# The sliding-window keys, values and first queries as a fifth pair of the last FoX period

## What is computed

```python
h = rmsnorm(x); z = h @ w_in          # FoX q, k, v, f | SWA q, k, v | gates g_fox, g_swa
# branch A (FoX): 8 heads of 64, causal, logits + sum of log forget gates
o_A = softmax(q @ k.T * SCALE + cum_q - cum_k) @ v
# branch B (SWA): 8 query heads, 2 key/value heads, a band of 3 chunks of 64, sinks, relative bias
o_B = sink_softmax(q @ k.T * SCALE + bias) @ v
merged = sigmoid(g_fox) * (o_A @ w_proj_fox) + sigmoid(g_swa) * (o_B @ w_proj_swa)
x = x + rmsnorm(merged @ w_o)         # then a ConvFFN over 2816 features
```

## Time and profile before

| | |
|---|---|
| median of 3 runs | 1749.28 us (1748.65 to 1751.57) |
| the profiled execution | 1747.95 us |
| its span | 1746.0 us, mean granted clock 0.967 |
| PE busy | 1616.0 us (93%) |
| DVE / ACT / POOL busy | 982.8 / 434.3 / 577.6 us |
| DMA | 122.88 MB, mean 70 GB/s |

### The profile page before, as it was taken

The page is one execution under the profiler, slowest core; times in us unless marked ns, Lnnn a source line. Parts: engine busy times, 40 slices in busy tenths (PEclk is TensorE's granted clock), DMA queues, the critical chain, the costliest instruction groups (busy, mean ns, idle before and its releaser), DMA issues.

```text
span 1746.0 us, 24406 instructions
## 1 busy us (share of the span) xinstructions
PE 1616.0 (93%) x9375; PEld 1504.1 (86%) x9375; DVE 982.8 (56%) x1846; ACT 434.3 (25%) x914; POOL 577.6 (33%) x312
## 2 busy tenths in 40 slices
PE   5979999988889798967899999999999999999996
PEld 5879999988679798857787998998989989989895
DVE  6756757677432474758645465545445455454556
ACT  4133434345211153532223210100101101001013
POOL 6322213121113313116232333432543444324443
PEclk9989999999989999888999999999999999999998
DMA  5422212221334211124533111111211111112115
GB/s 183 83 78 62 74 49 76 61 66 34 109 100 164 67 46 53 42 78 145 186 109 99 28 49 34 51 48 36 60 36 48 48 36 49 47 36 60 48 37 101
DMA packets 129614, 122.88 MB, mean 70 GB/s; under 512 B 7453, under 2 KB 116377, under 8 KB 129537
## 3 DMA queue, kind: packets, MB, share of 16 engines
q1 hardware_dynamic: 93513, 66.38, 13.1%
q10 hardware_dynamic: 34824, 51.13, 9.4%
q0 software_dynamic: 1200, 4.33, 1.4%
HBM read 94.00 MB, written 27.92 MB: 70 GB/s over the span
## 4 chain that ended last, share of the span: by engine, by line
PE 82%; DVE 12%; DMA 2%; issue 1%; ACT 1%; POOL 0%; SPq 0%; ACTq 0%; DVEq 0%; POOLq 0%
PE bank L682 17%; PE bank L683 17%; PE bank L684 17%; PE bank L688 6%; PE bank L690 6%; PE bank L689 6%; PE bank L714 4%; PE bank L835 2%; DVE m L1972 1%; DVE ssb L1727 1%; DVE ssb L1711 1%; PE bank L806 1%; PE bank L805 1%; DVE m_l L1956 1%; DMA gm<-d_mfox 1%
## 5 line engine op out<-in xcount | busy, mean ns | idle before, releaser
L575 POOL TENSOR_TENSOR ring_h<-raw,att 128x1024 fp32r<-128x1024 f32 x108 | 207.7, 1924 | 1011.8 <-PE bank L684 833.6
L682 PE MATMUL bank<-m_h,ring_h 128*128 128x352 f32 x1056 | 340.7, 323 | 0.7 <-DVE m_l L1524 0.7
L683 PE MATMUL bank<-m_l,ring_h 128*128 128x352 f32 x1056 | 338.6, 321 | 0.0
L684 PE MATMUL bank<-m_h,ring_l 128*128 128x352 f32 x1056 | 338.4, 320 | 0.0
L576 POOL TENSOR_TENSOR ring_l<-raw,ring_h 128x1024 fp32r<-128x1024 f32 x108 | 290.0, 2686 | 8.5
L682 PE MATMUL bank<-ht_h,ring_h 128*128 128x352 f32 x840 | 280.4, 334 | 0.2 <-DVE vqn L1535 0.2
L684 PE MATMUL bank<-ht_h,ring_l 128*128 128x352 f32 x840 | 274.4, 327 | 0.0
L683 PE MATMUL bank<-ht_l,ring_h 128*128 128x352 f32 x840 | 274.0, 326 | 0.0
L682 PEld LDWEIGHTS bank<-m_h,ring_h 128*128 128x128 f32 x1056 | 198.1, 188 | 1.2 <-DVE m_l L1524 0.8
L683 PEld LDWEIGHTS bank<-m_l,ring_h 128*128 128x128 f32 x1056 | 198.4, 188 | 0.3
L684 PEld LDWEIGHTS bank<-m_h,ring_l 128*128 128x128 f32 x1056 | 198.0, 188 | 0.0
(11 more groups left out here) (280 smaller groups left out, 2670.7 us busy)
## 6 DMA issues: line engine op xcount, KB each, us to landing
raw<-in_w_up SPq DMA_DIRECT2D x44, 512.0 KB, 3.9
raw<-in_w_in SPq DMA_DIRECT2D x35, 512.0 KB, 4.0
raw<-in_w_down SPq DMA_DIRECT2D x22, 512.0 KB, 3.6
d_gate<-gst ACTq DMA_DIRECT2D x48, 176.0 KB, 1.9
gm<-d_gate ACTq DMA_DIRECT2D x8, 528.0 KB, 4.2
d_mfox<-mst ACTq DMA_DIRECT2D x8, 528.0 KB, 2.9
gm<-d_gate ACTq DMA_DIRECT2D x24, 176.0 KB, 2.5
gm<-d_mfox ACTq DMA_DIRECT2D x24, 176.0 KB, 2.9
```

The lines of the kernel that those rows point to most:

```text
L575: order.link(nc.gpsimd.tensor_tensor(high, src, zero.to_broadcast(list(src.shape)), ALU.add))
L682: nc.tensor.matmul(out, wh, xh, start=start, stop=False)
L683: nc.tensor.matmul(out, wh, xl, start=False, stop=False)
L684: return nc.tensor.matmul(out, wl, xh, start=False, stop=stop)
```

## The change

The SWA keys, values and queries 0 take the place of a fifth pair: `KEYS`, `VALUES` and `QUERIES` list five slabs, and the conditions `p < LAST` around the preparation of the next pair fall away. So the last period gets whole chunks as fillers, 15 in steps 0 to 15 (gate 6, `sk`, `sv`, `sq` 0, gate 7) and three in the drain (gate 8). Gate 9's chunk 0 stands behind the key transposes of the sample attention, chunks 1 and 2 behind its scores, and the three chunks of `sq` 1 behind the probability transposes of each group and behind the last values. The function `key_value_query_slabs`, its counterparts and `gate_half` are gone. The second head's preparation for SWA goes into the drain on ACT and DVE. The high parts of the four FoX outputs (`out_high`) move behind the second load of the sample attention, their low parts (`out_low`) behind its scores. The sample's tiles move to where the FoX tiles are free, one tile `past` holds first the cached keys and then the cached values, and the values of all four pairs get their own part of bank 7. The bias table is loaded at the start of the projection, ahead of the high parts of `sq` 1.

```diff
-        SLABS += [("gate", 2 * pair + 1), ("gate", 2 * pair + 2)]
-SLABS += [("gate", 9)] + [("wf", i) for i in range(4)] + [("sk", 0), ("sv", 0)]
-SLABS += [("sq", 0), ("sq", 1), ("gate", 10), ("gate", 11), ("gate", 12)]
+        SLABS += [("sk", 0), ("sv", 0), ("sq", 0), ("gate", 2 * pair + 1)]
+SLABS += [("gate", 8), ("gate", 9), ("sq", 1)] + [("wf", i) for i in range(4)]
+SLABS += [("gate", 10), ("gate", 11), ("gate", 12)]
...
     def fillers(p, s):
-        if p == LAST:
-            return []
...
-        return [] if s in (-1, 3) else [s if s < 3 else s - 1]
+        return [] if s in (-1, 3) or s > NU + 2 else [s if s < 3 else s - 1]
...
-                    if p == LAST and 1 <= s <= 18:
-                        gate_half(SLAB["gate", 2 * p + (s - 1) // 6], (s - 1) % 6)
-                    if p < LAST and s == K_ROWS:
+                    if s == K_ROWS:
...
             n = SLAB["gate", 9]
-            dense_chunk(n, 0)
-            dense_chunk(n, 1)
             pe.wait_ge(smp_keys, 16 * 2)
...
+            dense_chunk(n, 0)
             pe.wait_ge(misc_dve, MD_QBD)
...
+            dense_chunk(n, 1)
             dense_chunk(n, 2)
-            pe.wait_ge(smp_in, 16 * 10)
+            pe.wait_ge(smp_in, 16 * 2)
             for g in range(2):
                 pe.wait_ge(p_ready, U_SMP + g + 1)
...
+                dense_chunk(SLAB["sq", 1], g)
                 pe.wait_ge(t_free, T_SMP + 8 + 2 * g + 2)
...
+            dense_chunk(SLAB["sq", 1], 2)
...
-            key_value_query_slabs(S_SK)
+            pe.wait_ge(kq_ready, 2 * PAIRS + 2)
+            pe.wait_ge(v_ready, 2 * PAIRS + 2)
             for g in range(KVH):
-                for i in range(g == 0, 2):
+                for i in range(2 * g):
```

More of the change, by code:

```diff
@@ L57 @@
 SLAB = {name: n for n, name in enumerate(SLABS)}
-S_F, S_WF, S_SK, S_SV = SLAB["f", 0], SLAB["wf", 0], SLAB["sk", 0], SLAB["sv", 0]
+S_F, S_WF = SLAB["f", 0], SLAB["wf", 0]
+KEYS = [SLAB["fk", pair] for pair in range(PAIRS)] + [SLAB["sk", 0]]
+VALUES = [SLAB["fv", pair] for pair in range(PAIRS)] + [SLAB["sv", 0]]
+QUERIES = [SLAB["fq", pair] for pair in range(PAIRS)] + [SLAB["sq", 0]]
 S_WS, S_WO, S_FFN = SLAB["ws", 0], SLAB["wo", 0], len(SLABS)
@@ L118, in program @@
     tails, _ = place("tails", [P, 4, FT])
-    qs, _ = place("qs", [P, PAIRS, DEC])
+    qs, _ = place("qs", [P, 2 * PAIRS, DEC])
     smallf, _ = place("smallf", [P, 24])
@@ L764, in row_tiles @@
                                           for t in tiles])
[L766 to L794, removed]
             def scores(p, u):
@@ L1239, in _ @@
             act.dma_start(fl_s[0, 0], lfn[0:DEC, NT, :]).then_inc(outs2, 16)
+            for ds, cache in ((sk_s, cache_swa_k), (sv_s, cache_swa_v)):
+                act.dma_start(ds[0, 0, 0:WIN - DEC], cache[0, 0, DEC:]).then_inc(outs2, 16)
             head_values(0, 0)
@@ L1306, in _ @@
-            fox_sample_load(smp_in, vns, cache_fox_v, fv_s)
-            for h in range(HEADS):
-                act.dma_start(nsc[DEC * (h % 4):DEC * (h % 4) + DEC, h // 4, :],
-                              d_cum[h:h + 1, SEQ:].to_broadcast([DEC, SKEYS])).then_inc(smp_in, 16)
+                    if p < LAST and s == 9:
+                        decay_load(p + 1, 0)
+                    if s == 9 or s == 10:
+                        head_keys(p + 1, 0, s - 9)
+                    if s == K_ROWS + 1:
+                        rows_out(p + 1, 0)
@@ new lines, in _ @@
+                    if s == V_ROWS + 1:
+                        rows_out(p + 1, 1)
+                    if s == 14:
+                        head_queries(p + 1, 0)
+                    if s == 15:
+                        head_values(p + 1, 0)
+                    if s == NU:
+                        act.wait_ge(s_free, S_FOX)
+                        past_load(smp_keys, cache_fox_k)
+                    if s == NU or s == NU + 1:
+                        head_keys(PAIRS, 1, s - NU)
+                    if s == NU + 1:
+                        fresh_load(smp_keys, fk_s)
+                        for h in range(HEADS):
+                            act.dma_start(nsc[DEC * (h % 4):DEC * (h % 4) + DEC, h // 4, :],
+                                          d_cum[h:h + 1, SEQ:].to_broadcast([DEC, SKEYS])).then_inc(smp_cum, 16)
@@ L1311, in _ @@
+            out_high(3)
             gate_store(9, 1)
@@ L1327, in _ @@
             gate_load(1)
+            act.dma_start(bias[:, :, :], bass.AP(tensor=d_rel.tensor, offset=P - 1,
+                                                 ap=[[RELS - 1, P], [P * RELS, HEADS], [1, SPAN]])).then_inc(bias_in, 16)
+            for c in range(3):
+                query_highs(SLAB["sq", 1], c, qsw, 2, qs[:, PAIRS + 1, :])
             def mfox_store(j):
@@ L1800, in _ @@
                 V.tensor_scalar(att[:, 2 + g:3 + g], att[:, 0:1], -1.0, None, ALU.mult).then_inc(mx_ready, 1)
+            for i in range(PAIRS):
+                out_low(i)
             for g in range(2):
```

269 lines of the change are left out of this document (113 added, 156 removed).

## The result

The change runs in 1718.51 us (median of 4 runs, 1716.19 to 1719.94), against 1750.42 us for the kernel before, run beside it (median of 4 runs, 1748.65 to 1751.83): a ratio of 0.9823 with a 95% interval of 0.9807 to 0.984, a gain of some 1.8% that is well clear of the spread of the runs. The prediction was 1721.8 in a range of 1713 to 1731. The profiled execution took 1718.52 us with a span of 1716.7, so between the two profiled executions the span fell by 1746.0 - 1716.7 = 29.3 us, where the sum of the prediction had 27.5.

A forecast was written before the change was run, and what follows sets the result against it. TensorE, 82% of the chain, was taken as the bound, with gains only where it waits or runs at its lower clock. 21.7 + 4.2 + 2.8 - 2.0 - 54.2 = -27.5 from 1749.28 gave 1721.8 us, range 1713 to 1731.

The forecast's parts named there:

- Step 1: Last FoX period: same work as the third period, so that one's 93.29 us in place of 71.64, +21.7 us.
- Step 2: Drain: three whole chunks in place of halves, a 1.59 us wait covered; 11.87 becomes 16.1, +4.2 us.
- Step 3: Sample attention: 11.6 us of added chunks, less covered waits and lower clock, plus clock fall, late copies, banks: +2.8 us.
- step 6: The rest: early cache-to-output copies, ot_h/ot_l passes under two sample attention chunks, smaller mask, moved buffers: costed at nothing.
- Step 4: FoX projection: a query chunk directly before it wins back half of 4.1 us at the lower clock, -2.0 us.
- Step 5: Before the first SWA score: all 59.42 us go, leaving about 5.2 of product, store, memsets and marker, -54.2 us.
- A: Sample attention: all covers hold, no clock fall, late copies or bank waits; 4.6 us less, 1717.2 us; chance 0.15.
- B: Sample attention: clock also falls in key transposes and scores, two more falls of 2.0 us, 1725.8 us; chance 0.15.
- C: Sample attention: gain given back, exponentials and probabilities each late by a chunk; stage 55.4, total 1730.6 us; chance 0.12.
- D: Last FoX period: the moved chunks are not hidden, 29.0 us instead of 21.7, total 1729.1 us; chance 0.05.
- E: Key transposes to projection: clock stays at 1.2 GHz, adding 36.3 us, total 1758.1 us; chance 0.03.
- F: First SWA score: something else sets it, 20 us or more later, total about 1749 us; chance 0.02.

The follow-up runs named there:

- Experiment 6: The changed kernel with the last FoX period's first three chunks one step later each, step 0 left bare: 1724.42 us.
- experiment 1: The changed kernel with TensorE's sample attention order as before and the three queries 1 chunks together behind the last values: 1737.63 us.
- experiment 3: The changed kernel with gate 9's chunk 0 in quarters between the key transposes and chunk 1 ahead of the scores: 1723.97 us.
- experiment 8: The kernel of experiment 3 with GpSimd's split of the second query slab held until VectorE has scaled the first sample probabilities: 1725.59 us.
- experiment 2: The changed kernel with bias corners and queries marker moved into the projection and the first SWA group's chunks one step earlier: 1715.35 us.
- experiment 9: The kernel of experiment 7 with the first SWA group's chunks back in steps 1 to 9, as in the change: 1711.97 us.
- experiment 4: The changed kernel with DVE scaling the second group's probabilities right behind the first group's: 1715.08 us.
- experiment 7: The changed kernel with the edits of experiment 2, experiment 3 and experiment 4 together and DVE's four ot_l passes spread out: 1710.34 us.

## Why the prediction was right, point by point

- **Step 1, last period (+21.7): right**, 93.32 for 93.29. A stage that has become the same list of instructions as another takes the other's time. Experiment 6 shows how little slack that has: three chunks put one step later cost 3.5 us in the period alone.
- **Step 2, drain (+4.2): right**, 3.9. The wait of 1.59 us on the last transposed probabilities is gone.
- **Step 3, sample attention (+2.8): the mechanism right, four terms too large.** It came out at +0.1. Key copies were put at 1.8 + 1.5 us and cost 2.1 (0.86, 0.61, 0.61). ACT's eight decay-row issues did stand in the way as described, and took 4.70 us, not 3.6, since one of them took 1.37: they ran from 478.86 to 483.56, the drain's last values ended at 482.67, and ACT's fold of them began at 483.67. But the third drain chunk covered most of it. The banks were put at 1.1 and cost 0.72 (waits of 0.57 and 0.15), the second group's probabilities at 1.7 and cost 1.42. The clock's fall of 2.0 us was 1.6 (5.48 us for the chunk in place of 3.86), and its place was wrong: behind the key transposes, not between the query chunks. That is 2.3 of the 2.7 us. The covers of 3.2, 1.6, 1.0 and 1.2 us held in full. The price of a chunk at the lower clock was put at 7.7 us, twice 3.86. In the rows of gate 9's first chunk the matmuls start 0.294 us apart at clock 0.50 and 0.160 at 1.00, so that a whole chunk at the lower clock would be about 7.1 us (an estimate, 24 x 0.294). The sum did not use the 7.7.
- **The stretching of DVE under GpSimd's split** was seen in the right row and put in the wrong place. I looked for it at DVE's query lows, which took their normal 1.22 us beside the split at 486.66. There it was the split's first pass that was long, 2.42 us in place of 1.89. It strikes the ot_l passes and the scaling, which the prediction held to be covered at no cost (step 6). They were covered in the change only because two chunks behind the scores kept the split away until 510.18 us, 1.5 us after the scaling had ended. Experiments 1, 3 and 8 show that this was no safe zero.
- **Step 4, projection (-2.0): right**, -1.9, clock 1.00 from its start.
- **Step 5, chain ahead of SWA (-54.2): right**, 5.17 us for 5.2, made of the store's landing and DVE's 1.5 us behind it, as described. The first SWA blocks started at the lower clock, as described (0.74 over 576 to 586 us). Experiments 2 and 9 show that it all lay on the path, and that no more than some 3 us of it can be had back with nine chunks.
- **Step 6 and the start (0):** the start was 1.7 us later. The change's code does not reach there, and other kernels with the same code up to the last period start it as early as 375.64. The rows of the last section put the difference down to the clock between 110 and 120 us.
- **The rivals.** A (1717.2) is nearest by time, but its premise failed: the clock did fall, and the copies and banks were late, if by less than in my sum. B put a fall in the key transposes and was right there, but it had three falls and there was one. The Trainium skill, "TensorE: Matmul & The Clock Gate", Part 4, says that transposes do not count as busy matmuls do. The place of the fall and the third experiment's 1.00 with dense quarters between the transposes agree with that. The pauses went with the transposes there, so the two are not told apart. C did not come in the change: the largest wait on the sample probabilities was 1.42 us. But experiments 1 and 3 have it at 5.85 and 5.91, by the four ot_l passes that C names too, stretched by a split, and not by ACT's queue. D, E and F are out: 93.32 us, one fall, 5.17 us.

The span fell by 1.8 us more than the sum had: +1.7 at the start, -2.7 in the sample attention, and small ones of -0.3 in the drain, +0.1 in the projection and -0.5 behind the first SWA score (the rest is rounding). The +1.7 is chance and hid part of the error. Without it the sum would have been off by 3.5 us.

## What to carry to other kernels

When work is moved so that one stage becomes a copy of another, read that other stage's length and use it whole; it is the surest number of all. For the covers, count chunks against steps: a row of steps with one chunk fewer than it needs pays its bare step (here 2.9 to 3.3 us) at whichever end it falls. And when chunks are moved, follow what their end releases on the other engines (here the split of a slab) and look at what runs there beside it. A pass costed at nothing may be covered only as long as that release comes late.

## What the runs showed of the hardware

- **GpSimd and VectorE stretch each other, and a short pass suffers most.** Beside a split of 128x1024, four ot_l passes went from 4.62 to 6.32 us, and a scaling of 128x544 with one input in SBUF went from 0.51 to 2.39 us. It ended 0.3 us behind the split in both runs (519.25 after 518.94, 511.74 after 511.44). The split's two passes went from 1.89 and 2.34 to 2.08 and 3.20. The Trainium skill, "SBUF — State Buffer", section "SBUF: two separate sides", calls the pair of ports that the two share an exclusive lock, held for a whole instruction. If the scaling uses that pair, it would wait for the split's second pass to end and then take its 0.5 us. That the scaling does use it is not shown otherwise. The trace agrees with the waiting (2.39 us in place of 0.51), but the scaling ended 0.3 us behind the split, less than its own 0.5.
- **The clock's fall depends on small shifts.** With the same instructions in the same order on TensorE, the key transposes' waits of 2.1 us cost 1.6 us of lower clock, those of 2.3 us (experiment 4) about 1 us more. The gap between the query chunks kept 1.00 in the change and in experiment 2 and ended in a fall in experiment 6 (0.63). A wait that is removed can be given back this way, so a run of small work with pauses should carry a range and not a value.
- **The start is not the same from kernel to kernel.** Nine kernels with the same code up to the last period reach it at 375.64 to 377.49 us, so a difference of 2 us between two single runs says nothing by itself. The place is the stretch from 110 to 120 us, with a wait of 3.85 us in it. Its granted clock was 0.50 in the four kernels that start at 377.20 to 377.49 (the change, experiments 2, 6 and 8), 0.52 to 0.55 in the three at 376.50 to 376.87 (3, 7 and 9), and 0.67 in the two at 375.64 and 375.65 (1 and 4). TensorE's work from the matmul behind that wait (113.45 us in the change, 113.19 in the first experiment) to its transposes at 121.97 and 120.29 took 8.52 us in the one and 7.10 in the other, which is 1.4 of the 1.6 us between them. What sets the length of the fall is open. The window in the change and in the first experiment, in the columns of the earlier trace rows:

```profile
110.00:120.00 10.00, 6.55 (x24) 6.36 (x25) 7.45 (x18) 3.57 (x9) 0.87 (x1) 0.50 0.20 53
```

```profile
110.00:120.00 10.00, 6.80 (x35) 6.61 (x36) 7.20 (x18) 3.31 (x8) 0.61 (x1) 0.67 0.20 52
```

- **An issue on ACT's queue has no fixed length.** The eight decay-row issues took 0.442 to 0.453 us each in the kernel before. In the nine kernels that have them in the drain the median is 0.44 to 0.46 us, but the longest takes 1.29 to 1.71, and all eight take 4.67 to 5.26. In experiments 4 and 6 the first key copy came later by just what the eight took more (0.28 and 0.56 us). Why one is long is open.
